# Ten couples of weight tiles by seven block products in a stage of their own, and two weight tiles a turn in the convolution stage

## The reference, cut to what matters

```
h    = rmsnorm(x, norm_pre1) * (1 + sc1) + sh1
proj = h @ w_in                     # bg, cg, ua, q, k, v, r, lr, ga, gb
y_a  = bg * (conv_b + sum(conv_w[j] * ext[j : j + T]))        # ext = history, cg * ua
log_a = log_sigmoid(lr @ w_a2 + b_a) / 16
o    = gla_recurrence(q, k, v, log_a, state)                  # 4 heads
y_b  = rmsnorm(o) * silu(r)
x   += g1 * rmsnorm((sigmoid(ga) * y_a + sigmoid(gb) * y_b) @ w_out)
a, g = split(h2 @ w_up);  f = (gelu(dwconv3(a)) * g) @ w_down;  x += g2 * rmsnorm(f)
```

## Time and profile before

| what | value |
|---|---|
| time, median of 3 runs (lowest to highest) | 980.48 us (980.03 to 981.25) |
| the profiled execution: time, span in the trace | 982.61 us, 980.9 us |
| PE busy (share of span) | 963.1 us (98%) |
| DVE, ACT, POOL busy | 564.9, 434.2, 222.4 us |
| mean granted TensorE clock | 0.998 of full |
| data moved by DMA | 115.58 MB |

### The profile page before, as it was taken

One profiled execution on the slowest core, in us unless ns is written; L12 is line 12 of the kernel. 1 busy time (PEld: TensorE's weight loads), 2 busy tenths in 40 slices (PEclk: granted clock), 3 DMA queues, 4 the chain that ended last, 5 costly groups with the idle time before them and its releaser, 6 DMA issues.

```text
span 980.9 us, 18498 instructions
## 1 busy us (share of the span) xinstructions
PE 963.1 (98%) x7599; PEld 875.2 (89%) x7599; DVE 564.9 (58%) x842; ACT 434.2 (44%) x692; POOL 222.4 (23%) x121
## 2 busy tenths in 40 slices
PE   5999999999999999999999999999999999999997
PEld 4889888989999999999898889999999999888886
DVE  2511205476565655345348589998999988660204
ACT  4535333134343324444444365655565556633212
POOL 3033532243333333333254000000000000013430
PEclk9999999999999999999999999999999999999999
DMA  9676353798466657545438023133323332422212
GB/s 330 229 103 190 108 86 87 156 97 150 147 144 165 141 131 139 67 137 152 102 120 242 1 84 88 46 107 99 96 87 95 100 97 75 121 74 86 87 52 96
DMA packets 145028, 115.58 MB, mean 118 GB/s; under 512 B 11225, under 2 KB 121585, under 8 KB 144945
## 3 DMA queue, kind: packets, MB, share of 16 engines
q1 hardware_dynamic: 144849, 114.38, 46.5%
q10 hardware_dynamic: 96, 0.04, 0.0%
HBM read 107.02 MB, written 7.35 MB: 117 GB/s over the span
## 4 chain that ended last, share of the span: by engine, by line
PE 95%; DVE 2%; ACT 1%; issue 1%; DMA 1%; SPq 0%; DVEq 0%; ACTq 0%
PE pair L2150 39%; PE pair L2567 20%; PE pair L2256 17%; PE pair L2524 5%; PE pair L2140 2%; PE pair L2337 1%; PE pair L2310 1%; PE pair L2080 1%; DMA x_tok<-in_x_prompt 1%; PE pair L2248 1%; PE pair L2400 1%; PE pair L2389 1%; PE pair L2249 1%; PE pair L2250 1%; PE pair L2247 1%
## 5 line engine op out<-in xcount | busy, mean ns | idle before, releaser
L933 POOL TENSOR_TENSOR w_lo<-raw,w_hi 128x1024 fp32r<-128x1024 f32 x53 | 129.2, 2439 | 537.6 <-ACT w_hi L1007 537.6
L2150 PE MATMUL pair<-h_hi,w_hi 128*128 128x288 f32 x944 | 213.7, 302 | 0.1
L2150 PE MATMUL pair<-h_hi,w_lo 128*128 128x288 f32 x944 | 207.4, 296 | 0.9 <-issue 0.9
L2150 PE MATMUL pair<-h_lo,w_hi 128*128 128x288 f32 x944 | 206.8, 295 | 0.0
L2150 PEld LDWEIGHTS pair<-h_hi,w_hi 128*128 128x128 f32 x944 | 153.2, 189 | 18.4 <-issue 16.7
L2150 PEld LDWEIGHTS pair<-h_hi,w_lo 128*128 128x128 f32 x944 | 153.5, 188 | 1.1 <-issue 1.1
L2150 PEld LDWEIGHTS pair<-h_lo,w_hi 128*128 128x128 f32 x944 | 153.4, 188 | 0.0
L1007 ACT ACTIVATE w_hi<-raw 128x1024 fp32r<-128x1024 f32 x66 | 69.6, 1057 | 161.7 <-PE pair L2250 80.2
L933 POOL TENSOR_TENSOR w_lo<-raw_c,w_hi 128x1024 fp32r<-128x1024 f32 x24 | 69.1, 2883 | 125.3 <-ACT w_hi L1007 125.3
L2567 PE MATMUL pair<-t_hi,w_hi 128*128 128x288 f32 x304 | 90.1, 296 | 0.7 <-ACT u_buf L1282 0.7
L2567 PE MATMUL pair<-t_lo,w_hi 128*128 128x288 f32 x304 | 89.7, 295 | 0.0
(11 more groups left out here) (361 smaller groups left out, 1751.3 us busy)
## 6 DMA issues: line engine op xcount, KB each, us to landing
raw_c<-in_w_ada SPq DMA_DIRECT2D x32, 512.0 KB, 5.1
raw<-in_w_in SPq DMA_DIRECT2D x224, 64.0 KB, 3.2
raw_c<-in_w_in SPq DMA_DIRECT2D x192, 64.0 KB, 3.7
raw<-in_w_up SPq DMA_DIRECT2D x24, 512.0 KB, 3.8
raw<-in_w_down SPq DMA_DIRECT2D x22, 512.0 KB, 3.7
raw_up<-in_w_up SPq DMA_DIRECT2D x20, 512.0 KB, 3.8
ada_first<-in_w_ada SPq DMA_DIRECT2D x16, 512.0 KB, 9.6
raw<-in_w_in SPq DMA_DIRECT2D x8, 512.0 KB, 4.8
```

Of the source, the lines that this page charges most:

```text
L933: pool.tensor_tensor(lo, raw_tile(n)[:, :], hi.bitcast(F32), ALU.subtract).then_inc(S("w_lo_done"), 1)
L2150: ins = pe.matmul(bank[pair][:, half, 0:HALF], w[:, i, :], x[:, i, HALF * half:HALF * half + HALF], start=i == 0 and p == 0, stop=i == KT ...
```

## The change

The four query tiles become two couples, and the gate tiles bg and ga of all eight channel blocks become eight couples (ga_j, bg_j). These ten couples stand in a new stage between the keys and V, each by seven block products. Their weight sums and all their low parts are made on DVE (POOL makes none until V); the four token factors are made on DVE and ACT ahead of the stage. The sigmoid of ga is taken there, and `early_gate` leaves y_a = bg * sigmoid(ga). SP loads two tiles for each couple in 16 pieces of 64 KB.

A turn of C1 keeps the tiles cg and ua, each cut in two halves, so that its items, pairs and mod_back stand between half tiles. The history copy, the first tap and the tail copies of the convolution go from DVE to ACT. DVE does the level's products ahead of the convolution and its two sums around the taps. At the end of a turn `conv_gate` multiplies y_a by the convolution's result. The sigmoid in C1, with its two table loads a turn, is gone. The stacked copy of the sample tokens (`h_smp_hl`) moves to other memory and is made after the last couple.

```diff
+EARLY = HEADS // 2 + KT
+TILE_K, TILE_E, TILE_V = 0, HEADS, HEADS + 4 * EARLY
 TILE_C1 = TILE_V + 8
-TILE_C2 = TILE_C1 + 4 * KT
+TILE_C2 = TILE_C1 + 2 * KT
...
+            def load_early(c, x):
+                if c < 2:
+                    cols = IN_Q + DK * (2 * c + x)
+                    sp.wait_ge(S("w_lo_done"), 2 * c + 2)
+                else:
+                    cols = (IN_GA, IN_BG)[x] + P * (c - 2)
+                    sp.wait_ge(S("w_lo_done"), early_fill(c - 2, 2 + x) + 1)
+                dst, src = kc(early_raw(c, x)), in_cols(cols)
+                for i in range(KT):
+                    sp.dma_start(dst[:, i, :], src[:, i, :]).then_inc(S(early_landed[c, x][0]), 16)
+            for c in range(EARLY):
+                for x in range(2):
+                    load_early(c, x)
...
+            def early_high(c, slot):
+                if slot in (0, 3):
+                    name, count = early_landed[c, slot // 3]
+                    act.wait_ge(S(name), count)
+                else:
+                    act.wait_ge(S("s_add"), 4 + 4 * c + 2 * slot)
+                act.wait_ge(S("ring_free"), early_fill(c, slot) - 3)
...
+            for c in range(EARLY):
+                n = c + 1
+                if n < EARLY:
+                    early_high(n, 0)
+                else:
+                    high(TILE_V)
+                early_u2(c)
+                early_p5(c)
+                if n < EARLY:
+                    early_high(n, 1)
+                else:
+                    high(TILE_V + 1)
+                if c >= 2:
+                    gate_sigmoid(c)
+                if n < EARLY:
+                    early_high(n, 2)
+                    early_u1(n)
+                    if c < 2:
+                        queries_out(c)
+                    early_high(n, 3)
+                    if c in (1, 2):
+                        decay_abs(c + 1)
+                else:
+                    high(TILE_V + 2)
+            act.wait_ge(S("ring_free"), TILE_V)
...
             for j in range(KT):
-                n = TILE_C1 + 4 * j
+                n = TILE_C1 + 2 * j
                 high(n + 3)
+                mix_history(j)
                 act.wait_ge(S("ring_free"), n + 1)
                 if j > 0:
                     act.wait_ge(S("u_done"), 3 * j)
                 act.activation(halves(buf_a[:, :]), out2(c1_pair(j, 0)), ACT.Copy).then_inc(S("cg_done"), 1)
                 high(n + 4)
-                high(n + 5)
                 if j + 1 < KT:
                     qd_exp(act, j + 1)
+                    if j > 0:
+                        kd_exp(act, j + 1)
                 else:
                     act.wait_ge(S("level_set"), KT)
                     act.activation(suf[:, :, :], suf[:, :, :], ACT.Exp, scale=TAU_INV).then_inc(S("exps"), 1)
+                mix_first_tap(j)
+                mix_tails(j)
...
+            factor(0, b12, b11)
+            dve.wait_ge(S("s_add"), 1)
+            factor(1, b22, th_32[0][:, :, :])
+            factor(2, b22, b12)
+            dve.wait_ge(S("s_add"), 2)
+            factor(3, b21, th_32[1][:, :, :])
+            decay_min(0)
+            early_sums12(0)
+            dve.wait_ge(S("w_lo_done"), TILE_E)
+            early_low(0, 0)
+            factor_low(1)
+            early_low(0, 1)
+            factor_low(0)
+            early_sums34(0)
+            early_low(0, 2)
+            factor_low(2)
+            factor_low(3)
+            for c in range(EARLY):
+                n = c + 1
+                early_c11(c)
+                early_low(c, 3)
+                if n < EARLY:
+                    early_sums12(n)
+                    early_low(n, 0)
+                if c in (1, 2, 3):
+                    decay_min(c)
+                early_c22(c)
+                if n < EARLY:
+                    early_low(n, 1)
+                early_c12(c)
+                if n < EARLY:
+                    early_sums34(n)
+                if c >= 2:
+                    early_gate(c)
+                if n < EARLY:
+                    early_low(n, 2)
...
+            for j in range(KT):
+                for e in (0, 2, 4):
+                    for i in after_tile(j, e):
+                        take_item(dve, i)
                 if j + 1 < KT:
-                    dve_level(dve, j + 1)
-                else:
+                    level_products(dve, j + 1)
+                else:
                     dve.wait_ge(S("exps"), 1)
                     dve.tensor_tensor(k[:, :, :], k[:, :, :], suf[:, :, :], ALU.mult).then_inc(S("decayed"), 1)
-                    dve.wait_ge(S("exps"), 2)
-                    dve.tensor_tensor(q[:, :, :], q[:, :, :], pre[:, :, :], ALU.mult).then_inc(S("decayed"), 1)
+                conv_input(j)
                 for i in after_tile(j, 6):
                     take_item(dve, i)
+                if j + 1 < KT:
+                    level_suffix(dve, j + 1)
+                mix_taps(j)
+                if j + 1 < KT:
+                    level_prefix(dve, j + 1)
                 if j > 0:
                     take_mod(dve, j - 1)
-                dve.wait_ge(S("t_done"), 3 * (j + 1))
-                dve.wait_ge(S("sga_done"), j + 1)
-                dve.tensor_tensor(y_a[:, j, :], y_a[:, j, :], buf_b[:, :], ALU.mult).then_inc(S("ya_done"), 1)
+                conv_gate(j)
                 for i in after_tile(j, 7):
                     take_item(dve, i)
                 dve.wait_ge(S("ada_mm"), 2 * (j + 1))
                 if j > 0:
                     dve.wait_ge(S("back"), j)
                 dve.tensor_copy(rows_ada[:, :], one_bank(6)[:, :]).then_inc(S("rows_ada"), 1)
+            dve.wait_ge(S("exps"), 2)
+            dve.tensor_tensor(q[:, :, :], q[:, :, :], pre[:, :, :], ALU.mult).then_inc(S("decayed"), 1)
...
+            def early_products(c):
+                b11, b21, b22 = (quarters(h_hi, h_lo, k, t) for k, t in ((0, 0), (1, 0), (1, 1)))
+                t1, t2, t3, t4 = ((th_hi[i][:, :, :], th_lo[i][:, :, :]) for i in range(4))
+                a, b, cc, d = ((w_hi[i], w_lo[i]) for i in range(4))
+                x, y, z = 2 + c % 2, 4, 5
+                def factors_made(n):
+                    if c == 0:
+                        pe.wait_ge(S("h_lo_done"), KT + n)
+                pe.wait_ge(S("w_lo_done"), early_fill(c, 0) + 1)
+                if c < 2:
+                    pe.wait_ge(S("kq_done"), 2)
+                elif c < 4:
+                    pe.wait_ge(S("kq_done"), HEADS + 3 * (c - 1))
+                else:
+                    pe.wait_ge(S("ya_done"), 2 * (c - 3))
+                block_product(a, 0, b11, x, True).then_inc(S("x_mm"), 1)
+                if c == 0:
+                    pe.wait_ge(S("kq_done"), 3)
+                else:
+                    pe.wait_ge(S("c_sum"), 3 * c - 2)
+                block_product(a, 1, b21, y, True).then_inc(S("ring_free"), 1)
+                pe.wait_ge(S("w_lo_done"), early_fill(c, 1) + 1)
+                pe.wait_ge(S("a_done"), 3 * c + 1)
+                factors_made(1)
+                block_product(b, 1, t2, x, False).then_inc(S("x_mm"), 1)
+                if c > 0:
+                    pe.wait_ge(S("c_sum"), 3 * c)
+                factors_made(2)
+                block_product(b, 0, t1, z, True).then_inc(S("ring_free"), 1)
+                pe.wait_ge(S("w_lo_done"), early_fill(c, 2) + 1)
+                pe.wait_ge(S("a_done"), 3 * c + 2)
+                factors_made(3)
+                block_product(cc, 0, t3, x, False).then_inc(S("x_mm"), 1)
+                pe.wait_ge(S("a_done"), 3 * c + 3)
+                block_product(cc, 1, b22, z, False).then_inc(S("ring_free"), 1)
+                pe.wait_ge(S("w_lo_done"), early_fill(c, 3) + 1)
+                pe.wait_ge(S("c_sum"), 3 * c + 2)
+                factors_made(4)
+                block_product(d, 0, t4, x, False).then_inc(S("ring_free"), 1)
+            for c in range(EARLY):
+                early_products(c)
+                if c in (1, 2):
+                    z_rows(c + 1)
+                elif c == 4:
                     late_parameters()
-                if n in Z_BEHIND:
-                    z_rows(Z_BEHIND.index(n))
...
                 for e in range(8):
                     if e % 2 == 0:
-                        n = TILE_C1 + 4 * j + e // 2
-                        pe.wait_ge(S("w_lo_done"), n + 1)
-                        if n < TILE_C1 + 2:
-                            pe.wait_ge(S("v_summed"), n - TILE_C1 + 1)
-                        before = 4 * j + e // 2 - 3
-                        if before >= 0:
-                            name, count = (("cg_done", 1), ("u_done", 3), ("t_done", 3), ("sga_done", 1))[before % 4]
-                            pe.wait_ge(S(name), count * (before // 4 + 1))
-                        channel_tile(kc(w_hi[n % 4]), kc(w_lo[n % 4]), c1_pair(j, e // 2), (h_hi, h_lo))
+                        x = e // 4
+                        n = TILE_C1 + 2 * j + x
```

(48 more changed lines are left out.)

396 lines of the change are left out of this document (240 added, 156 removed).

## The result

The changed kernel takes 1020.18 us (median of 4 runs, 1019.11 to 1021.07) against 980.49: a ratio of 1.0404, interval 1.0386 to 1.0422, 39.7 us slower. Forecast were 998 us, and 1010 at most.

What follows compares the result with a forecast made beforehand. PE's matmul count was taken as the bound. C1 -77.2, couples +89.3, queries -3.4 and ends +3.2 gave +11.9 us, 992.4 on the median; 6 for clock falls made 998 us, range 975 to 1010.

Steps and rivals of the forecast that it cites:

- the floor: Whole kernel: twenty tiles at 6.43 us become ten couples at 11.16; worth -17.0 us if PE waits nowhere.
- the couples' 11.16 us: Early stage: each steady couple costs 11.16 us, as in the FFN; eight gate couples 89.3 us, two query couples 22.3.
- C1's stops: Heads of seven C1 turns: PE waits for DVE's mod, 4.3 us once, 5.3 three times, 2.9 three times.
- POOL's low part in front of pre: C1 turns: POOL asks during DVE's taps and goes next, so pre waits 2.4 us once a turn.
- the front's 1.5: Front of the early stage: the first couple's seventh product waits for a DVE sum, +1.5 us.
- turn 1 started where it was laid out: C1: turn 1's first item starts 24.4 us after C1 does; PE alone would be there at 20.1.
- the sum: Whole kernel: C1 -77.2, couples +89.3, queries -3.4, ends +3.2, in all +11.9 us, then 6 for the clock.
- between no fall (0) and seven (12) I take 6: Clock behind C1's seven stops: each fall to half speed adds up to 1.7 us; 6 us taken in all.
- all four ... together lie between 0 and 6. I take 3.2: Early and late ends: key tiles' low part +0.6, first couple's sum +1.5, stacked copy +0.3, end of C1 +0.8.
- The rival on transfers: Transfers or early stage hold PE up: slow C1 turns give 1010 to 1022, late couples +5; mostly 1003 to 1012; chance 0.12.
- the layout: Stage times built row by row: V's start 88.0 us later; C1 163.8 us, turns 22.3 or 19.7.
- the rivals: Alternatives to the forecast (0.65): POOL misses the gap 0.17, PE stays the bound 0.06, transfers or early stage 0.12.

Runs made afterwards that it cites:

- the best version: All mends plus `rows_ada` ahead of the gate on DVE, on the changed kernel: 970.60 us, ratio 0.9906 to the kernel before.
- The fillers: Changed kernel plus matmuls nobody reads ahead of the first item of C1's turns 1 to 7, all waits kept: 1008.62 us, ratio 1.0285 to the kernel before.
- The one edit: Changed kernel with ACT's stacked copy of the sample tokens ahead of the high part of V's third tile: 1013.37 us, ratio 1.0331 to the kernel before.
- the run with the later low part: Changed kernel with POOL's low part of the tile behind the next put off until DVE's pre is done: 997.24 us, ratio 1.0163 to the kernel before.

## Why the prediction was wrong

Right were the floor (-17 us by matmuls; -16 of PE's busy time in the best version), the couples' 11.16 us, the place and the mechanism of C1's stops, their lengths (26.3 for 28.9), POOL's low part in front of pre in the second tap (3.5 us for the 3.6 forecast), the front's 1.5 (1.4), and the direction. That turn 1 started where it was laid out (24.6 us into C1 for 24.4) was in part luck: PE came there 1.0 us later than laid out and stood 0.8 us less.

Wrong by stage, in the spans of the two profiled executions, which differ by +37.6 us where the sum was +17.9 (the medians differ by 39.7, because the profiled execution of before lay 2 us above its median):

- **"between no fall (0) and seven (12) I take 6"** is the step that failed in C1, with its upper bound. Every stop halved the clock, and two of them for nearly twice the 3.4 us that one stop at the start of the program had shown, so that C1 took 177.2 instead of 163.8 us: 13.4 for 6. From turn 1 on, a turn was 1.2 to 2.4 us longer than laid out, where a fall had been priced at up to 1.7. The fillers show it: same work on the other engines, clock up, C1 10.6 us less. I had one row for the length of a fall and took it for all.
- **"all four ... together lie between 0 and 6. I take 3.2"** failed for the end of the early stage. The stacked copy was costed by its own length (0.3); what stands ahead of it on ACT waits for a transfer, 4.2 us, and the clock fell there too (V's stage 5.8 us longer than before). The one edit took 6.8 us off.
- **The early stage's couples "at 11.16 us"** held but for one. The rival on transfers, put at 0.12 and in the range's upper end, came in addition to the forecast and not in its place: 5.3 us of stop, and 5.7 us at half clock behind it, which lose some 2.9. The rest of the stage ran about 1 us under the layout, so V's start came 7.1 us later than laid out. I had read 96 GB/s from 206 to 216 us as what full DMA engines give; that stretch holds block 3's tiles beside a modulation tile, and the rows above show 54 to 68 for those tiles alone, while other blocks came at 100 to 112 with the engines as full (158 to 166 us after).

In these three the excess is 7.4 us (13.4 less the 6), 5.5 (V's stage 5.8, less the 0.3 of the copy) and 7.1. Together, less 0.3 behind C2's start, they are the 19.7 us between forecast and measured span. I had set the rivals beside the forecast as if only one could hold; the stops here add up, and each brings its fall of the clock.

The Trainium skill, TensorE: Matmul & The Clock Gate, section "HAM oscillation", has each burst behind a wait start at 1.2 GHz again; these rows agree, at stops down to 2.7 us, and show that the rule spoke against the change more strongly than I let it. The Trainium skill, SBUF — State Buffer, section "Who interferes with whom", has two-input DVE instructions exclude GpSimd; the row of POOL's 2.93 us behind a tap agrees for scalar_tensor_tensor, which no row of before showed.

## What to carry to other kernels

When a stage gets shorter, lay out the loop through the other engines that used to hide in it, row by row: here half the matmuls left a turn, and a loop of 19.7 to 22.3 us came to light where PE needed 17. Price a stop of PE as its length plus a stretch at half clock, and look at what stands ahead of the awaited row in its engine's queue, since a copy of 0.6 us behind a late tile costs what the tile costs. A stop that is removed uncovers the next gate of the same queue, so that only the mends together (in C1 mod, POOL's low part, item copies and `rows_ada`, in the early stage buffers and the order of ACT and of V's loads) turned +39.7 into -10.0 us. Ask of a slow stretch of transfers which columns it reads: these were slow in the trace of before already.

## What the runs showed of the hardware that was not expected

- Transfers of one block's tiles (128 columns each, pieces of 64 KB) ran at 53 to 55 GB/s with the DMA engines full, where other blocks ran at 100 to 112. The slow stretch moved with the columns, from 104 to 120 us to 148 to 168. In the order of issue the other tiles of block 3 lie in slow stretches too: cg and ua in C1 after the change (40 to 69 GB/s from 256 to 264 us), all four in the kernel before (44 to 86 between 196 and 234 us).
- Behind a stop the clock stayed at 0.50 for about 3 us in some turns and 6.3 in another (291.9 and 316.0, stops of 5.28 and 5.20 us). What decides between the two was not tried.
- A stop of 2.18 us was followed by half clock as well (at 330.5 in the run with the later low part: 0.86, 0.50 and 0.79 in the three stretches of 2 us from 330 on).
